# Two activations of the second feed-forward layer's block down moved one place forward in ScalarE's order

## The reference

```python
def swiglu(h, w1, w3, w2):
    return (jax.nn.silu(h @ w1) * (h @ w3)) @ w2
...
h = modulate(rms_norm(x, g_ffn2[l]), sh3, sc3)
x = x + 0.5 * gt3[:, None, :] * swiglu(h, w1_b[l], w3_b[l], w2_b[l])
return rms_norm(x, g_final)
```

## Time and profile before

| | us |
|---|---|
| median of 3 runs | 2141.44 (2141.2 to 2144.02) |
| profiled execution, its own time | 2140.3 |
| span of the profiled execution | 2138.5 |
| PE busy | 2085.2 (98%) |
| POOL busy | 1302.5 (61%) |
| DVE busy | 1217.6 (57%) |
| ACT busy | 721.3 (34%) |

### The profile page before, as it was taken

The page is one execution under the profiler, slowest core; times in us unless marked ns, Lnnn a source line. Parts: engine busy times, 40 slices in busy tenths (PEclk is TensorE's granted clock), DMA queues, the critical chain, the costliest instruction groups (busy, mean ns, idle before and its releaser), DMA issues.

```text
span 2138.5 us, 26768 instructions
## 1 busy us (share of the span) xinstructions
PE 2085.2 (98%) x9554; PEld 1714.7 (80%) x9554; DVE 1217.6 (57%) x1417; ACT 721.3 (34%) x1106; POOL 1302.5 (61%) x896
## 2 busy tenths in 40 slices
PE   7999999999999999999999999999999999999998
PEld 4788888888888778888888888887887878787887
DVE  6965445363456787777874654339446272635556
ACT  5633231323223453333333420116323323332334
POOL 1565563737456367766666765535768787778860
PEclk8999999999999999999999999999999999999999
DMA  8132424251322332233234444311111122111212
GB/s 297 60 118 74 143 69 148 59 165 51 112 85 64 114 109 94 80 105 96 90 93 158 162 153 148 98 49 40 60 40 51 48 59 60 50 50 49 63 47 79
DMA packets 224859, 197.23 MB, mean 92 GB/s; under 512 B 17028, under 2 KB 193328, under 8 KB 223600
## 3 DMA queue, kind: packets, MB, share of 16 engines
q1 hardware_dynamic: 200112, 154.42, 23.3%
q10 hardware_dynamic: 24640, 41.40, 6.0%
HBM read 169.45 MB, written 25.17 MB: 91 GB/s over the span
## 4 chain that ended last, share of the span: by engine, by line
PE 83%; POOL 6%; DVE 4%; ACT 3%; DMA 2%; issue 1%; ACTq 1%; SPq 0%; DVEq 0%; POOLq 0%
PE unit_b L1469 10%; PE unit_d L1469 9%; PE unit_b L1190 9%; PE unit_a L1469 7%; PE unit_c L1469 7%; PE unit_a L1190 6%; PE unit_c L1258 5%; PE unit_d L1258 5%; PE unit_b L1065 3%; PE unit_a L1065 2%; PE unit_d L1065 2%; PE unit_c L1065 2%; POOL raw L983 2%; POOL w_low L979 2%; DMA ada_first<-in_w_ada 1%
## 5 line engine op out<-in xcount | busy, mean ns | idle before, releaser
L951 POOL TENSOR_TENSOR w_low<-raw,w_high 128x512 fp32r<-128x512 f32 x200 | 269.2, 1346 | 173.5 <-ACT w_high L1852 159.9
L1852 ACT ACTIVATE w_high<-raw 128x512 fp32r<-128x512 f32 x200 | 125.6, 631 | 330.9 <-PE unit_b L1469 128.8
L921 POOL TENSOR_TENSOR w_low<-raw,w_high 128x512 fp32r<-128x512 f32 x64 | 98.7, 1545 | 193.2 <-ACT w_high L1809 193.2
L902 POOL TENSOR_TENSOR w_low<-raw,w_high 128x512 fp32r<-128x512 f32 x80 | 118.1, 1477 | 114.1 <-ACT w_high L2081 110.3
L869 POOL TENSOR_TENSOR w_high<-raw,ones 128x512 fp32r<-128x512 f32 x44 | 59.4, 1349 | 98.0 <-PE unit_b L1065 33.4
L2081 ACT ACTIVATE w_high<-raw 128x512 fp32r<-128x512 f32 x100 | 62.1, 629 | 159.7 <-PE unit_b L1190 117.7
L979 POOL TENSOR_TENSOR w_low<-raw,w_high 128x512 fp32r<-128x512 f32 x56 | 91.2, 1628 | 36.4 <-ACT w_high L1900 34.9
L2690 DVE TENSOR_TENSOR fg_two<-fg_one,unit_b 128x512 f32<-128x512 f32 x48 | 33.0, 687 | 130.9 <-PE unit_b L1469 130.6
L1190 PE MATMUL unit_b<-t_high,w_high 128*128 128x512 f32 x240 | 93.7, 390 | 3.5 <-POOL w_low L902 2.8
L1469 PE MATMUL unit_d<-t_high,w_high 128*128 128x512 f32 x240 | 93.6, 390 | 0.1
L1190 PE MATMUL unit_b<-t_low,w_high 128*128 128x512 f32 x240 | 93.4, 389 | 0.0
(11 more groups left out here) (583 smaller groups left out, 6328.7 us busy)
## 6 DMA issues: line engine op xcount, KB each, us to landing
raw<-in_w_a SPq DMA_DIRECT2D x66, 512.0 KB, 4.5
raw<-in_w_b SPq DMA_DIRECT2D x66, 512.0 KB, 3.9
raw<-in_w_in SPq DMA_DIRECT2D x44, 512.0 KB, 3.8
ada_ring<-in_w_ada SPq DMA_DIRECT2D x84, 256.0 KB, 3.5
ada_first<-in_w_ada SPq DMA_DIRECT2D x8, 1024.0 KB, 20.4
sg_kept<-s ACTq DMA_DIRECT2D x16, 512.0 KB, 2.7
s<-sg_kept ACTq DMA_DIRECT2D x16, 512.0 KB, 3.4
ada_ring_last<-in_w_ada SPq DMA_DIRECT2D x28, 256.0 KB, 3.5
```

Of the source, the lines that this page charges most:

```text
L902: pool.tensor_tensor(low_, mixer_plain(q, slots), high.bitcast(F32), ALU.subtract).then_inc(mixer.operand_low, 1)
L921: pool.tensor_tensor(low_, plain, high.bitcast(F32), ALU.subtract).then_inc(f.operand_low, 1)
L951: pool.tensor_tensor(low_, weight_plain(PRODUCTS[q][0], slots, f.n), high.bitcast(F32), ALU.subtract).then_inc(f.operand_low, 1)
L1852: act.activation(operand((here.ring[n] + q) % 4)[0], weight_plain(PRODUCTS[q][0], slots, f.n), ACT.Copy).then_inc(f.operand_high, 1)
```

## The change

In ACT's order of a block down the high part of part 3 comes ahead of unit 6, where it came ahead of unit 7, and that of part 4 ahead of unit 8, where it came ahead of unit 9. Parts 2, 5 and 6 stay. No instruction is added or removed, no wait is changed, and the orders of the other engines are the same.

```diff
                 def block_down(here):
 
                     for u in range(DOWN_UNITS):
-                        if u >= 5 and u % 2 == 1:
-                            block_part(here, u // 2)
+                        if u in (5, 6, 8, 11, 13):
+                            block_part(here, (5, 6, 8, 11, 13).index(u) + 2)
                         block_unit_high(here, u)
```

## The result

The changed kernel takes 2129.54 us (median of 5 runs, 2128.6 to 2132.9), the kernel before 2142.16 (5 runs, 2141.2 to 2145.88): a ratio of 0.9937, 95% interval 0.9926 to 0.9948. By the ratio that is 13.5 us less, by the medians 12.6; 12.3 less and a time of 2129.1 had been forecast. The two profiled executions have spans of 2127.1 and 2138.5 us.

The account below looks back on a forecast made before the run. PE was taken as the bound, losing 15.5 us to waits and low clock at products 3 and 4. Gains of 12.3 us off the profiled 2140.3 gave 2128.0, plus 1.1 for the median: 2129.1 us, range 2125.9 to 2134.5.

Parts of the forecast that it names:

- The rival without the exchange: DVE and POOL share without waiting: product 3 starts 2.33 us earlier, every PE wait goes, 2125.9 us; chance 0.10.
- order A: At product 4, POOL's sum 4 goes ahead of DVE's low part of part 4: 12.3 us gained, 2129.1 us; chance 0.53.
- Order B: At product 4, DVE's low part goes ahead of POOL's sum 4: 0.91 us less gain each time, 2132.8 us; chance 0.18.
- The sum, 12.3 us: Gain over four block downs at product 4's start: 3.27, 2.87 twice, and 3.27 less 0.01.
- order B with the low clock: DVE first at sum 4, and product 3 still 7.20 us long in two block downs: 2133.1 us; clock falls, chance 0.12.
- no fall behind the short waits: Granted clock stays 1.0 through the block downs, with about 0.2 and 0.6 us of wait left ahead of products 3 and 4.
- The rival of a long low stretch: Shorter waits bring a long low-clock stretch to each block down, PE losing 5.1 us four times: 2149.5 us; chance 0.02.
- No new wait: Behind product 4 PE gets no wait; DVE's reads are done 0.4 us before product 5 wants them.

Follow-up runs that it names:

- e4: The changed kernel with DVE making sum 4 behind product 3's reads, not product 0's: 2126.55 us, ratio 0.9924 to the kernel before.
- e5: The kernel before, ACT's order kept, with DVE making sum 4 behind product 3's reads, not product 0's: ratio 0.9979 to the kernel before.
- e6: The changed kernel with DVE making part 4's low part ahead of all reads of product 2, not between them: ratio 0.9951 to the kernel before.
- e7: The changed kernel with DVE making the low parts of parts 3 and 4 behind all four reads of the product: ratio 0.9958 to the kernel before.
- e1: The changed kernel with part 4 back ahead of unit 9, so only part 3 moved: ratio 1.0004 to the kernel before.
- e2: The changed kernel with part 3 back ahead of unit 7, so only part 4 moved: ratio 0.9983 to the kernel before.
- e3: The changed kernel with part 3 already ahead of unit 5: ratio 1.0019 to the kernel before.
- e8: The kernel before, unchanged, run once more for another trace: 2145.91 us.

## Why the prediction was right

**What PE loses, and to whom.** 15.5 us of waits and low clock were counted. e4, where every wait is gone, has block downs 15.5 us shorter (168.2 to 152.7). That ACT's queue caused them, not POOL alone, is shown by e4 against e5: DVE's order is the same and POOL's sum 3 starts at the same place (10.8 us into the block down) and takes the same 2.4 us, only the order on ACT differs, and that is 11.2 us.

**Product 3.** Forecast: the low part of part 3 starts when DVE is done with two reads, waits for sum 3, takes about 2.0 us; product 3 2.10 us earlier. Measured: 2.10 us long, and product 3 is 7.80 - 5.71 = 2.09 earlier. PE's wait ahead of it is 0.08 us at most, where 0.1 to 0.3 was forecast. The rival without the exchange, 2.33, is out, by this, by e4's 2.41 us sum and by e6. By the Trainium skill ("SBUF — State Buffer", Who interferes with whom) a DVE instruction with two SBUF inputs contends with a GpSimd instruction that reads SBUF, and issue order decides who is blocked. The traces agree in both directions: DVE 1.21 against 2.10 and 3.37, POOL 2.4 against 3.4.

**Product 4.** Forecast: order A by 0.09 us, sum 4 at 2.37, the low part 3.3, a wait of up to 0.5. Measured: A in all four block downs, 2.39, 3.37, 0.35. Product 4 starts 11.79 us behind product 2 (1624.77 - 1612.98), where it was 15.00: 3.21 earlier, forecast 3.27. Order B, forced in e6, started product 4 0.8 us later where 0.91 stood, and cost 0.73 a block down. The choice of A rested on 0.09 us of a sum whose other terms were off by as much, so that it came out is partly luck; in the traces POOL is first by 0.05 to 0.11 us, each time.

**The sum, 12.3 us, was a little large.** The block downs gained 3.04, 2.80, 2.79 and 3.05, 11.7 in all. About half of the missing 0.6 is a term that stood at nothing: a product that follows a wait takes 5.57 to 5.61 us to the next one's start, not 5.44. In block downs 1 and 4 of the kernel before, product 4 had no wait ahead of it (the clock had filled that time) and took 5.44; with the change it has one. The other half is that product 4 starts 0.05 to 0.08 us later than summed in each block down. The time itself, 2129.54 against the 2129.1 forecast, is closer than the parts of the sum: the spans differ by 11.4, the medians by 12.6, and the interval of the ratio, 11.1 to 15.9 us, takes in both the 11.7 and the 12.3. That half of a microsecond is luck. One rival was added up wrong: order B with the low clock comes to 2133.3 us by the prediction's own terms, not 2133.1, which changes nothing.

**The clock.** Forecast: no fall behind the short waits. Neither trace of the change has one in its block downs, nor have e4 to e7, with waits of up to 1.2 us. Behind waits of 2.2 to 2.5 us it fell in 13 of 24 (before 2 and 3 of 4, e1's kernel 3 and 3, e2 and e3 1 each). The rival of a long low stretch found nothing for it. Behind such a wait a product took 1.63 us more with a fall than without, but in the kernel before most of that lay where product 4 would have waited anyway: its block downs with a fall are only 0.3 us longer (42.20 and 42.17 against 41.91). So the clock is 0.6 us of the 11.7 that the change brings. The Trainium skill ("TensorE: Matmul & The Clock Gate", Part 1), by which the low clock is the default that activity releases and the watch isn't tied to the kernel, agrees with falls that sit in other block downs from trace to trace (e8); the same kernel of e1 had them in the same three twice.

**Behind product 4.** No new wait, neither at product 5 nor in the next chunk, as forecast.

## What to carry to other kernels

Look not only at what an engine waits for but at what stands behind the waiting instruction in its queue; if something there has all its inputs, move it ahead, but only ahead of instructions that wait longer than it does (one place further and the kernel is slower than at the start, e3). Two such stalls in a row hang together: cured singly they gave -1.6 and 4.2 us, together 11.7, so a half that brings nothing doesn't refute the whole. And when two engines exclude each other, find the operation that isn't wanted soon (sum 4 here) and move it off the other's critical work; that took another 3.8 us off the four block downs for one changed digit.

## What the runs showed of the hardware

- DVE and POOL operations whose operands all lie in SBUF exclude each other for a whole instruction, and the record of the one that waits includes the wait. DVE's 128x1024 form took 1.21 us by itself, and 2.10 and 3.37 where it started under one of POOL's sums, each time ending 1.1 us behind it. DVE operations with one input from PSUM kept their 1.40 for two beside POOL's sum.
- A product that follows a wait takes 0.09 to 0.17 us longer than 5.44 to the next one's start, and a low clock behind the wait costs 1.63 us more. In e2 a block down with one wait of 2.2 us takes 40.57 us without a fall and 42.22 with one, against 38.08 for seven products of 5.44: the wait costs 2.5 or 4.1 us.
- The same program's trace ahead of the block downs varies more than the effect of some experiments. The changed kernel's block down 1 started at 1602.10 and 1604.68, that of before at 1601.38 and 1607.11. Part of it is the granted clock around 740 us, here in the two traces of before, first e8's, then the first one's (length, busy PE, PEld, DVE, ACT, POOL with their counts, granted clock, DMA share, GB/s):

```profile
735.00:760.00 25.00, 22.00 (x94) 16.13 (x93) 21.71 (x28) 16.90 (x26) 4.53 (x3) 0.80 0.69 220
```

```profile
735.00:760.00 25.00, 22.31 (x109) 17.09 (x109) 23.55 (x33) 20.80 (x32) 1.63 (x2) 0.93 0.68 219
```

  PE got through 94 records in the one and 109 in the other. By an estimate from the two clocks that is (0.93 - 0.80) x 25 = 3.3 of the 5.7 us by which these two differ. For effects of 1 us the length of the changed stretch in the trace, which repeats to 0.05 us where the clock doesn't fall, says more than a median of five runs.
